# Two row blocks of the modulation sums, moved from TensorE to ScalarE and GpSimd

## What is computed

```python
silu_c = jax.nn.silu(c)            # 1024 values
silu_cc = jax.nn.silu(c_ctx)       # 1024 values
for layer in range(2):
    mod = (silu_c @ w_mod[layer] + b_mod[layer])[:, None, :]     # w_mod[layer]: 1024 x 6144
    mod_c = silu_cc @ w_mod[layer] + b_mod[layer]
```

```python
def swiglu(x, w_gu, w_down):
    g, u = jnp.split(x @ w_gu, 2, axis=-1)      # w_gu: 1024 x 5632
    return (jax.nn.silu(g) * u) @ w_down        # w_down: 2816 x 1024
```

## Time and profile before

| | us |
|---|---|
| median of 3 runs | 1775.71 (1775.66 to 1775.8) |
| profiled execution | 1775.88 |
| its span | 1774.0 |
| TensorE busy | 1752.1 (99%) |
| VectorE busy | 1096.7 (62%) |
| ScalarE busy | 807.1 (45%) |
| GpSimd busy | 119.5 (7%) |

### The profile page before, as it was taken

The page is one execution under the profiler, slowest core; times in us unless marked ns, Lnnn a source line. Parts: engine busy times, 40 slices in busy tenths (PEclk is TensorE's granted clock), DMA queues, the critical chain, the costliest instruction groups (busy, mean ns, idle before and its releaser), DMA issues.

```text
span 1774.0 us, 25358 instructions
## 1 busy us (share of the span) xinstructions
PE 1752.1 (99%) x10293; PEld 1491.4 (84%) x10293; DVE 1096.7 (62%) x1381; ACT 807.1 (45%) x1048; POOL 119.5 (7%) x106
## 2 busy tenths in 40 slices
PE   8999999999999999999999999999999999999998
PEld 7888897788878888888877888888888989998886
DVE  6876576677787566754244467754327795576655
ACT  6544536554565334754233422223227465365554
POOL 3000101300002101010000100000001120000000
PEclk9999999999999999999999999999999999999999
DMA  9966588677544322023324478873324423656752
GB/s 282 278 220 231 166 301 320 166 213 212 184 142 137 119 72 71 25 60 110 101 77 119 119 213 239 241 240 110 113 71 149 143 72 94 197 162 190 210 193 94
DMA packets 313204, 286.38 MB, mean 161 GB/s; under 512 B 10681, under 2 KB 292275, under 8 KB 310032
## 3 DMA queue, kind: packets, MB, share of 16 engines
q1 hardware_dynamic: 309695, 279.67, 50.5%
q0 software_dynamic: 2208, 5.21, 1.0%
q10 hardware_dynamic: 1200, 0.07, 0.0%
HBM read 282.66 MB, written 2.13 MB: 161 GB/s over the span
## 4 chain that ended last, share of the span: by engine, by line
PE 90%; DVE 4%; ACT 2%; DMA 1%; SPq 1%; issue 1%; POOL 0%; ACTq 0%; DVEq 0%
PE PS L2390 18%; PE PS L2391 18%; PE PS L2392 18%; PE PS L2443 12%; PE PS L2447 6%; PE PS L2615 3%; PE PS L2617 3%; PE PS L2616 3%; PE PS L3134 2%; DVE WLO L1517 1%; DMA RAW<-in_ffn_w_gu_dram 1%; ACT WHI L881 1%; PE PS L3240 1%; PE PS L2676 1%; PE PS L3101 1%
## 5 line engine op out<-in xcount | busy, mean ns | idle before, releaser
L1517 DVE TENSOR_TENSOR WLO<-RAW,WHI 128x2048 fp32r<-128x2048 f32 (+1 forms) x210 | 479.9, 2288 | 305.8 <-ACT WHI L881 305.5
L881 ACT ACTIVATE WHI<-RAW 128x2048 fp32r<-128x2048 f32 (+1 forms) x211 | 397.4, 1885 | 243.8 <-PE PS L2392 144.0
L2390 PE MATMUL PS<-AHL,WHI 128*128 128x512 f32 (+1 forms) x1428 | 487.6, 341 | 0.4 <-DVE WLO L1517 0.3
L2392 PE MATMUL PS<-AHL,WLO 128*128 128x512 f32 (+1 forms) x1428 | 481.8, 337 | 0.0
L2391 PE MATMUL PS<-AHL,WHI 128*128 128x512 f32 (+1 forms) x1428 | 481.8, 337 | 0.0
L2443 PE MATMUL PS<-AHL,WHI 128*128 128x512 f32 x1021 | 323.6, 395 | 2.1 <-DVE WLO L1517 2.1
L2390 PEld LDWEIGHTS PS<-AHL,WHI 128*128 128x128 f32 x1428 | 270.8, 190 | 35.7 <-issue 6.6
L2392 PEld LDWEIGHTS PS<-AHL,WLO 128*128 128x128 f32 x1428 | 270.9, 190 | 29.0
L2391 PEld LDWEIGHTS PS<-AHL,WHI 128*128 128x128 f32 x1428 | 270.9, 190 | 28.7 <-issue 0.7
L2447 PE MATMUL PS<-AHL,WLO 128*128 128x256 f32 x1021 | 235.6, 280 | 0.0
L2443 PEld LDWEIGHTS PS<-AHL,WHI 128*128 128x128 f32 x1021 | 188.9, 188 | 46.2 <-issue 3.6
(11 more groups left out here) (367 smaller groups left out, 2182.5 us busy)
## 6 DMA issues: line engine op xcount, KB each, us to landing
RAW<-in_w_in_dram SPq DMA_DIRECT2D x98, 512.0 KB, 4.6
RAW<-in_w_gate_up_dram SPq DMA_DIRECT2D x88, 512.0 KB, 5.1
RAW<-in_ffn_w_gu_dram SPq DMA_DIRECT2D x84, 512.0 KB, 5.3
MRAW<-in_w_mod_dram SPq DMA_DIRECT2D x24, 1024.0 KB, 8.0
LRAW<-in_w_mod_dram SPq DMA_DIRECT2D x48, 512.0 KB, 4.8
RAW<-in_ffn_w_down_dram SPq DMA_DIRECT2D x44, 512.0 KB, 4.3
RAW<-in_w_down_dram SPq DMA_DIRECT2D x44, 512.0 KB, 4.2
RAW<-in_w_out_dram SPq DMA_DIRECT2D x24, 512.0 KB, 4.5
```

Of the source, the lines that this page charges most:

```text
L881: act.activation(WHI[:, c % RING, a:b], RAW[:, c % RING, a:b], ACT.Copy).then_inc(S("hi_done"), 1)
L1517: dve.tensor_tensor(WLO[:, c % RING, a:b], RAW[:, c % RING, a:b], WHI[:, c % RING, a:b].bitcast(F32), ALU.subtract)\
L2390: pe.matmul(out, whi, xhi, start=first, stop=False, skip_group_check=shared)
L2392: return pe.matmul(out, wlo, xhi, start=False, stop=last, skip_group_check=shared)
```

## The change

Row blocks 0 and 1 (steps 0 to 15) leave TensorE's list. Each is now handled in one feed-forward part: block 0 from chunk 9 of `ffn1_gu` to chunk 7 of `ffn1_dn`, block 1 in `ffn2_gu`, chunks 2 to 20. A unit n is half a step (128 rows, 1024 columns): ScalarE loads 512 KB on its own DMA queue (`pooled_load`), multiplies it by the column of each of the two Silu vectors (`pooled_products`, two activations of 128x1024), and GpSimd adds the products of units 2 to 15 to those of the first two (`pooled_adds`, 28 additions of 128x1024 a block). TensorE then sums over the 128 rows with 8 matmuls a block (`pooled_rows`), between the two turns of rows after `ffn1_dn`, and ahead of `ffn2_dn`. The eight steps of block 2 stay on TensorE: one after `b1_in`, two in the attention, five after `b1_out`. ScalarE's gate-and-up loop is written out in full, the bias tables are loaded after block 0's additions, and the filter tables are issued two chunks later in `ffn2_dn`, behind the wait for all sums.

```diff
-GU_MODS = 2
+POOLED = 8
+POOLED_UNITS = 2 * POOLED
+POOLED_ADDS = 2 * (POOLED_UNITS - 2)
+POOLED_AT = ((9, 10, 12, 13, 15, 16, 18, 19, 20, FT, FT + 1, FT + 2, FT + 3, FT + 5, FT + 6, FT + 7),
+             (2, 3, 4, 6, 7, 8, 10, 11, 12, 14, 15, 16, 17, 18, 19, 20))
+TURNED = 2 * POOLED
-                    if stage == "ffn2_dn" and j == 0:
+                    if stage == "ffn2_dn" and j == 2:
                         filter_tables(sp, 0)
@@ GpSimd
+            def pooled_adds(r):
+                for n in range(POOLED_UNITS):
+                    for v in range(2):
+                        pool.wait_ge(S("mod_row"), 2 * POOLED_UNITS * r + 2 * n + v + 1)
+                        if n >= 2:
+                            if n >= 4:
+                                pool.wait_ge(S("mod_acc"), POOLED_ADDS * r + 2 * (n - 4) + v + 1)
+                            pool.tensor_tensor(pooled_acc(n, v), pooled_acc(n, v), POOL_IN[n % 2][:, v, :, :], ALU.add)\
+                                .then_inc(S("mod_acc"), 1)
+            pooled_adds(0)
...
             add_squares(2, 4)
+            pooled_adds(1)
             tap_weights(0)
@@ ScalarE
+            def pooled_products(r, n):
+                turns = n // 2 + 1 + (mod_turns(MAIN - 1, n % 2) if r else 0)
+                act.wait_ge(S(f"mod_raw{n % 2}"), 16 * turns)
+                for v in range(2):
+                    if n >= 4:
+                        act.wait_ge(S("mod_acc"), POOLED_ADDS * r + 2 * (n - 4) + v + 1)
+                    at = 4 + 32 * (n // 2) + v
+                    act.activation(pooled_acc(n, v) if n < 2 else POOL_IN[n % 2][:, v, :, :], pooled_raw(n), ACT.Identity,
+                                   scale=SC[:, at:at + 1]).then_inc(S("mod_row"), 1)
+                if n + 2 < POOLED_UNITS:
+                    act.wait_ge(S("mod_row"), 2 * POOLED_UNITS * r + 2 * n + 2)
+                    pooled_load(r, n + 2)
...
+                    if j in POOLED_AT[inst]:
+                        pooled_products(inst, POOLED_AT[inst].index(j))
@@ TensorE
-                        modulation(*range(GU_MODS))
+            def pooled_rows(r):
+                pe.wait_ge(S("c_ev"), 4)
+                pe.wait_ge(S("mod_acc"), POOLED_ADDS * (r + 1))
+                for v in range(2):
+                    x = 2 * r + v
+                    for b in range(4):
+                        last = pe.matmul(PS[32 * b:32 * b + 32, 7, :], SEL[:, 7 - x:39 - x], MRAW[v][:, b, :], start=x == 0, stop=x == 3,
+                                         skip_group_check=True)
+                last.then_inc(S("mod_used"), 1)
...
+                if inst == 1:
+                    pooled_rows(1)
                 down_rows(f + "_dn", inst, SHI1, SLO1)
                 rows_turned(inst, 0)
-                modulation(FILLED)
+                pooled_rows(0)
                 rows_turned(inst, 1)
-                modulation(FILLED + 1, FILLED + 2)
...
-                modulation(*range(FILLED + 3, FILLED + 6))
+                modulation(TURNED)
```

More of the change, by code:

```diff
@@ L209, in mod_slot, with mod_used_by @@
 def mod_slot(t):
-    if t < FILLED + 6:
-        return t % 3
-    if t < GU_MODS + 17:
-        return 3 + (t - FILLED - 6) % 4
-    return t - GU_MODS - 17 if t < GU_MODS + 22 else (t - GU_MODS - 22) % 3
+    if t < AT_ATTENTION:
+        return 2
+    if t < AT_BORDER:
+        return 3 + (t - AT_ATTENTION) % 4
+    return t - AT_BORDER
+def mod_used_by(t):
+    return 2 + t - TURNED
 def later_turn(i):
-    return sum(mod_slot(t) == i % LATER_RING for t in range(MAIN)) + i // LATER_RING + 1
+    return mod_turns(MAIN - 1, i % LATER_RING) + (POOLED if i % LATER_RING < 2 else 0) + i // LATER_RING + 1
 def later_accs(i):
@@ L231, in later_steps, with mod_turns @@
 def later_steps(i):
-    return sum(len(later_accs(n)) for n in range(i + 1))
-def mod_turns(t):
-    return sum(mod_slot(u) == mod_slot(t) for u in range(t + 1))
+    return 2 * POOLED_ADDS + sum(len(later_accs(n)) for n in range(i + 1))
+MAIN_USED = mod_used_by(MAIN - 1) + 1
+def mod_turns(t, slot=None):
+    slot = mod_slot(t) if slot is None else slot
+    return (POOLED if slot < 2 else 0) + sum(mod_slot(u) == slot for u in range(TURNED, t + 1))
 def mod_before(t):
-    return max((u for u in range(t) if mod_slot(u) == mod_slot(t)), default=None)
+    return max((u for u in range(TURNED, t) if mod_slot(u) == mod_slot(t)), default=None)
 def squares_before(n_norm):
@@ L668, in body @@
                         sp.dma_start(CS[:, :, :], d["ctx_2"][0].rearrange("(t p) n -> p t n", p=P)).then_inc(S("in_rows"), 16)
-                    if layer == 0 and 6 <= j < GU_MODS + 6:
-                        mod_load(j - 6)
                     if layer == 1 and j == 0:
-                        for t in range(GU_MODS + 17, GU_MODS + 22):
+                        for t in range(AT_BORDER, MAIN):
                             mod_load(t)
@@ L731, in _ @@
             plain("b1_in", d["w_in"][0])
-            for t in range(FILLED + 4, FILLED + 6):
-                mod_load(t)
             plain("b1_out", d["w_out"][0])
-            for t in range(FILLED + 8, GU_MODS + 17):
+            for t in range(AT_ATTENTION + 2, AT_BORDER):
                 mod_load(t)
@@ L895, in context_squares @@
             def context_squares():
+                act.wait_ge(S("mod_acc"), 2 * POOLED_ADDS)
                 act.wait_ge(S("c_ev"), 4)
@@ L1022, in body @@
                         act.activation(PHI[:, :, :], P32[:, :, :], ACT.Copy).then_inc(S("p_hi"), 1)
-                steps(act, stage, body, tail=1, least=6)
+                    if j == (6, 0)[inst]:
+                        if inst == 0:
+                            act.wait_ge(S("sc"), 2)
+                        else:
+                            act.wait_ge(S("mod_used"), mod_used_by(MAIN - 1))
+                        for n in range(2):
+                            pooled_load(inst, n)
+                    if j in POOLED_AT[inst]:
+                        pooled_products(inst, POOLED_AT[inst].index(j))
+                for j in range(FT):
+                    body(None, j, FIRST[stage] + j)
             act.dma_start(IDENT[:, :], d["ident"]).then_inc(S("in_x"), 16)
@@ L2571, in among_downs @@
             def among_downs(inst, i, j):
-                if inst == 0 and 3 <= j < DN_MODS + 3:
-                    modulation(GU_MODS + j - 3)
                 if inst == 1:
@@ L2915, in _ @@
                 mixed(2)
-                modulation(FILLED + 14, FILLED + 15)
                 mixed(3)
@@ L2924, in _ @@
                                ready=wait_k("act_lo", 2 * KT) if j == 0 else None)
-                modulation(GU_MODS + 17)
+                modulation(AT_BORDER)
                 norm_sums(3, 2, SQ1)
-                modulation(GU_MODS + 18)
+                modulation(AT_BORDER + 1)
                 norm_rows(3)
-                modulation(*range(GU_MODS + 19, GU_MODS + 22))
+                modulation(*range(AT_BORDER + 2, MAIN))
             pe.wait_ge(S("p_lo"), 1)
```

63 lines of the change are left out of this document (34 added, 29 removed).

## The result

The changed kernel takes **1833.9 us** in the median (1832.5 to 1834.9, 5 runs) against 1775.8 us (1775.7 to 1776.3, 5 runs) for the kernel before: a ratio of 1.0325, 95% interval 1.0314 to 1.0336. The profiled execution took 1832.6 us, its span is 1830.8. The forecast was 1818.0, its range 1798 to 1833. The direction was right, and the time lies 0.9 us above the range: of 58 us lost, 42 were foreseen.

What follows compares the result with a forecast made beforehand. TensorE, 90% of the chain, was taken to bound the kernel. Terms 12.2 + 9.3 + 26.3 - 1.85 - 0.95 + 0.4 - 3.1 = +42.3 us on the 1775.71 median gave 1818.0 us, range 1798 to 1833.

Steps and rivals of the forecast that it cites:

- The exclusion and its price: GpSimd additions and VectorE operations with two SBUF inputs never overlap; each addition holds VectorE 2.26 us, 7.56 per two-addition chunk.
- WLO means well over 2.29 in both stages: Expected sign: VectorE's low part of the weights lengthens beyond 2.29 us; if it stays 2.29 during additions, the exclusion is wrong.
- First gate-and-up, 12.2 late: VectorE's lateness builds up over seven chunks with additions, so TensorE begins the first down stage 12.2 us later.
- First down stage, 9.3: Low part of the hidden state comes too late for chunks 4 to 8: five stalls of about 1.9, +9.3 us.
- the forecast's stall at chunk 4: First down stage: first of five stalls, the low part of the hidden state 1.8 us too late for chunk 4.
- The move costs nothing: Block weights in half-size pieces over ScalarE's queue cost 0 while each unit's load, issued two units ahead, lands in time.
- Second gate-and-up, 26.3: Lateness reaches 20.8 us at chunk 20; TensorE then waits for the last sums before the second down stage: +26.3 us.
- Rival 1, the clock: TensorE's clock falls in stalls before both down stages: 5.4 us each, 10.8 in all, less where VectorE bounds; chance a quarter.
- Attention, -3.1: Steps removed from TensorE in the attention and after its projection save 3.1 us, with 2.6 and 9.3 as ends.
- a late ScalarE: ScalarE becomes late too, 0.35 us a unit over 28 units: 1828 us; chance 0.25 shared with the clock.

Runs made afterwards that it cites:

- The moved block: Changed kernel with GpSimd's loads of the bias tables moved from behind block 0's last addition to the first linear of b1: 1826.35 us.
- the two cut kernels: Changed kernel with block 1's unit 2 additions cut to 8 columns, 1831.9 us; the same with ScalarE's products of its units 0 to 2 cut too, 1828.6 us.

## Why the prediction was off, step by step

The mechanism was right: GpSimd's additions hold off VectorE, and TensorE pays at the ends of the stages. What failed are three terms of the sum. The second gate-and-up was priced as a stage that is steady from its first chunk (6.2 us too little), the move of the loads at nothing (5.45 us), and the clock at 0 (3.5 us). They make 15.2 us; between the 42.3 of the sum and the 57.2 measured lie 14.9, for the smaller misses have both signs.

- **The exclusion and its price: right.** A chunk with two additions takes 7.57 us (forecast 7.56), one without 3.86 (3.8). The sum from PSUM is untouched, as said. One sign was told wrongly: the prediction's "WLO means well over 2.29 in both stages" holds for the down stage only (4.49). In the gate-and-up HB and the product by the root do the waiting and WLO keeps 2.29; the sentence behind it, that 2.29 would refute the exclusion, was too quick.
- **First gate-and-up, 12.2 late: nearly right.** Net +9.2 and not +10.35. The difference is there before the additions: the last WLO ahead of them runs 2.89 us earlier than in the kernel before (91.68 and 94.57), where the two steps are worth 1.85. In six kernels with this same stage it runs at 91.68 to 92.53, and in the five of them without spare matmuls the down stage begins at 152.39 to 153.28, so up to 0.9 of the 1.1 is what one execution differs from another by.
- **First down stage, 9.3: right in all, in part by another way.** 8.75 us are lost up to chunk 8: four stalls of 1.76 us (1.5 of waiting each) at chunks 5 to 8, and 1.7 in the first chunk at the lower clock (7.21 us, in the kernel before 5.52) in place of the forecast's stall at chunk 4. In the kernel with 20 spare matmuls, whose clock is full there, the stalls are five, at chunks 4 to 8, as foreseen. What the forecast did not have is 5.45 us of waiting for ZROWS behind it: 8.75 + 5.45 - 0.99 = 13.2 of the 13.3 measured.
- **"The move costs nothing" for loads: failed, at another load.** The units' loads stayed hidden but for one wait of ScalarE, 1.64 us at the second block's first unit. But moving a wait moves every DMA queued behind it: the tables' loads came behind the last addition, and the additions' own lateness pushed them onto the first linear's weights. The moved block shows it, 5.45 us.
- **Second gate-and-up, 26.3: the largest miss, 8.0.** The sum began it as a steady stage, with ScalarE's products inside its 2.95 us of idle time and a first unit that costs 0.25 after the next chunk. Its start is a catch-up, in which neither engine has idle time: WLO at chunk 20 is 6.2 us later than forecast, and the two cut kernels give back 6.2 where the model has 0.3. The sums ran at the lower clock (1.72). That makes 7.6 to 7.9 of the 8.0.
- **Rival 1, the clock: right in kind, a third in size.** The granted clock fell to half at the two long waits, at the turn of the rows and once in the attention (0.50 in 307 to 309). It cost nothing at the first down stage, where VectorE set the pace behind it (the rival's own reservation), 1.8 at the turn and 1.72 at the second block's sums: 3.5 where the rival had 10.8. It was held off the sum because no row of the kernel before showed it; where it costs, it costs little because only the first work behind each wait runs at the lower level (to 156 at the first down stage, not to the chunk's end). That the turn of the rows would have such a wait at all, the rival did not foresee.
- **Attention, -3.1: -2.5 measured** with a fall of the clock in it.
- **The range** ended at 1833, made of the clock or a late ScalarE, one of them at a time. Clock, catch-up and loads came together: the clock and the tables' loads follow from the same lateness, and the catch-up stands beside them in every execution. Effects that share a cause do not take turns. That the time came out within 1 us of the range's end is partly luck: of the clock's 10.8 us 3.5 came, and the tables' loads, which no case of the prediction has, filled up the rest.

## What to carry to other kernels

Work moved to GpSimd beside VectorE is free only while each piece, times the two-input operations of VectorE that let it in, fits into VectorE's idle time of the chunk; if it does not, shorter pieces help a little, and giving the work to VectorE itself can be cheaper (2.47 us a unit against 3.7 to 4.4). Reckon idle time stage by stage: at a stage's start, where the helpers catch up, there is none. When work comes late, follow also the DMAs that are queued behind it and the waits in which TensorE's clock falls, and add these up instead of choosing one; but count the clock only where TensorE, and no slower engine, sets the pace behind the wait.

## What the runs showed of the hardware

- Four memsets of 128x512 on GpSimd (0.53 us each) run beside VectorE's two-input operations without lengthening them (0.42, 2.29), while an addition of 512 columns holds the next one off for 1.10 us and one of 1024 columns for 2.2.
- VectorE's two-input operations and GpSimd's additions alternate one by one where both wait: HB 0.42 to 2.63 and the product by the root 0.69 to 2.17 in every chunk with two additions of 1024 columns, 1.52 and 0.98 with two of 512.
- The length of a wait alone does not tell whether TensorE's granted clock falls. It fell in the waits of 12.8, 13.8 and 5.65 us (0.50 in 143 to 144, 0.53 in 500 to 508, 0.50 in 225 to 227), and around those of 4.8 and 2.6 us ahead of 18 and 20 spare matmuls, so that the first of these ran at 0.50. The wait of 5.1 us at the start and one of 2.9 us ahead of 96 spare matmuls left it at full.
- A clock at half behind a wait costs nothing to the stage's end when another engine sets the pace there: first down chunks of 5.66, 7.21 and 8.29 us in three kernels, and chunk 8 begins 0.14 or 0.15 us behind its SLO in all of them.
- The same list of TensorE's instructions at a granted clock of 1.00 runs its pairs of matmuls (512 and 256 columns) 0.347 or 0.353 us apart, and can change from one to the other within a stage.
- In a stretch of 12 us at a DMA share of 1.06 and 345 GB/s ScalarE waited 7.46 us for weights; without the tables' loads the share is 0.71 and TensorE's wait behind it 0.20 us and not 5.65.
- VectorE's multiply by a column and add, 128x1024 in f32, takes 1.28 us with both tensors in SBUF, like its 56 fellows in the later stages.
